# Seven quarter products in place of eight for 68 weight chunks, with weights in rings of 1024 columns

## The chip, the core and the metric

The kernel runs as one program on one NeuronCore of a Trainium2 chip. TensorE (PE) multiplies, VectorE (DVE), ScalarE (ACT) and GpSimd (POOL) do the element work, SyncE (SP) issues the DMAs. The metric is the time of one execution on the device in microseconds, median of several runs: 2743.62 before (2740.0 to 2743.9, 3 runs).

## The reference

One layer of a streaming encoder on x of shape (1, 512, 2048) in float32. Only the products matter here; norms, softmax, convolution and pooling stay as they are.

```python
h = rms_norm(x, norm_mix_pre[l])
z = h @ w_in[l]                              # 2048 x 3328, feeds four mixers A, B, C, D
...                                          # y_a, y_b, y_c, y_d: each mixer, then its own 512 x 2048 map
merged = jax.nn.sigmoid(h @ w_gate[l, 0] + b_gate[l, 0]) * y_a
merged = merged + jax.nn.sigmoid(h @ w_gate[l, 1] + b_gate[l, 1]) * y_b
merged = merged + jax.nn.sigmoid(h @ w_gate[l, 2] + b_gate[l, 2]) * y_c
merged = merged + jax.nn.sigmoid(h @ w_gate[l, 3] + b_gate[l, 3]) * y_d
x = x + rms_norm(merged @ w_o[l], norm_mix_post[l])
h2 = rms_norm(x, norm_ffn_pre[l])
gu = h2 @ w_ffn_in[l]                        # 2048 x 11264
f = (jax.nn.silu(gu[..., :D_FF]) * gu[..., D_FF:]) @ w_ffn_out[l]
x = x + rms_norm(f, norm_ffn_post[l])
```

## The kernel before

Everything is kept transposed: 128 channels on the partitions, the 512 positions on the free axis. A float32 number travels as a pair of float16 numbers, "hi" (rounded) and "lo" (the rest), and a product of two pairs is three float16 matmuls: hi by hi, hi by lo, lo by hi (`three`, lines 1058 to 1063). Each of the three matmuls loads its own 128 x 128 weights, although the first two use the same.

The weights come as **chunks** of 2048 rows by 256 columns, 2 MB in float32: 13 of `w_in`, then for each of 8 pairs of output tiles 4 gate chunks and one chunk of branch weights, 8 of `w_o`, 44 of `w_ffn_in` (each holds 128 gate columns and the 128 up columns that belong to them) and 32 smaller ones of `w_ffn_out` (11 row tiles each). A chunk passes four hands: SP loads it into one of two slots of `stage` (line 249), ACT makes hi (`hi`, line 416), DVE makes lo (`lo`, line 684), PE runs `gemm`: two output tiles of 128 x 512, each 16 row tiles times three matmuls, so 96 matmuls per chunk. ACT may overwrite a weight slot only when PE has finished the chunk before last (`chunk_done`), SP only when lo is made (`lo_ready`).

All waits are semaphores and each engine works its instructions in order. The repeating parts are hardware loops (`Fori`) on every engine: on PE one with 924 matmuls per turn for the pairs 1 to 6 (3 turns of 2 pairs), one with 192 for `w_o` (3 turns), one with 192 for `w_ffn_in` (20 turns of 2 chunks) and one with 264 for `w_ffn_out` (8 turns).

In the gate stage ACT takes the sigmoid out of PSUM, and DVE merges (`merge`, lines 917 and 921): branch product times gate, four added. In the FFN stage DVE scales both tiles (lines 1007 and 1010), ACT takes the silu (line 637), DVE multiplies (line 1017), ACT and DVE split the result into hi and lo (lines 642 and 1024). The two-step norms between the stages are where PE waits for others.

The matmuls themselves and the functions that the diff touches:

## Time and profile before

| | |
|---|---|
| time, median of 3 runs | 2743.62 us (2740.0 to 2743.9) |
| span of the profiled execution | 2739.6 us; the page gives no time of its own around it, the timed runs lie 0.4 to 4.3 us above |
| PE | busy 2693.0 us, 98%, 12452 matmul records |
| PE weight loads | busy 1233.7 us, 45% |
| DVE | busy 1034.3 us, 38% |
| ACT | busy 713.1 us, 26% |
| POOL | busy 105.7 us, 4% |
| HBM | 104 GB/s over the span |
| granted TensorE clock | 0.995 on average |

Engines work beside one another, so the shares don't add up. A matmul record is longer than its place in the pipeline: it is 380 ns for 512 columns while the next one starts 216 ns later, and the distance of two starts is what counts. "Idle before" a group says what the engine waited for.

### The profile page before, as it was taken

The page shows a single profiled execution, that of the slowest core. Times are in us where ns is not written, and L with a number is a line of the kernel's source. Part 1 is how long each engine was busy: PE and PEld are TensorE (multiplying, and loading weights), DVE is VectorE, ACT ScalarE, POOL GpSimd, SP SyncE. Part 2 cuts the span into 40 slices and gives each one's busy share as a digit, 9 for nine tenths or more (in the row PEclk, how much of TensorE's full clock was granted, in tenths as well). Part 3 has the DMA queues.
Part 4 walks back from the last instruction along what each step waited for, and adds up shares of the span by engine and source line. Part 5 has one row for each costly group of instructions (what it writes and reads, how often), then busy time and mean ns, then how long its engine had stood idle before and what let it go on. Part 6 is the DMA issues. An engine that isn't in the chain of part 4 may idle for free.

```text
span 2739.6 us, 28637 instructions
## 1 busy us (share of the span) xinstructions
PE 2693.0 (98%) x12452; PEld 1233.7 (45%) x12452; DVE 1034.3 (38%) x792; ACT 713.1 (26%) x537; POOL 105.7 (4%) x96
## 2 busy tenths in 40 slices
PE   7999999999999999999899999999999999999998
PEld 4444444444444444444444444444444444444443
DVE  8976534323323323321643333333333332222123
ACT  5226322222222222222432222222222222122221
POOL 0000020000000000011400000000000000000002
PEclk9999999999999999999999999999999999999999
DMA  5221222222222223242143223222222312222223
GB/s 227 98 93 62 93 87 106 103 87 108 102 90 97 110 87 117 98 165 106 60 156 122 92 92 114 101 92 103 111 92 95 119 63 106 105 102 90 103 105 122
DMA packets 23108, 286.39 MB, mean 105 GB/s; under 512 B 2560, under 2 KB 2688, under 8 KB 3968
## 3 DMA queue, kind: packets, MB, share of 16 engines
q1 hardware_dynamic: 23040, 285.37, 27.8%
q8 instruction: 57, 0.93, 0.1%
q14 instruction: 11, 0.09, 0.0%
HBM read 276.97 MB, written 8.39 MB: 104 GB/s over the span
## 4 chain that ended last, share of the span: by engine, by line
PE 96%; DVE 2%; issue 1%; ACT 0%; DMA 0%; DVEq 0%; POOL 0%; SPq 0%; ACTq 0%; POOLq 0%
PE psum L1061 31%; PE psum L1063 31%; PE psum L1062 31%; PE psum L1152 1%; PE psum L1177 0%; DVE region_b L982 0%; DVE region_a L971 0%; DVE wlo L694 0%; DVE stage L1049 0%; PE psum L1090 0%; PE psum L1163 0%; DMA region_b<-x_t 0%; DVE region_a L754 0%; DVE region_b L1044 0%; DVE work L743 0%
## 5 line engine op out<-in xcount | busy, mean ns | idle before, releaser
L684 DVE SCALAR_TENSOR_TENSOR wlo<-stage,whi 128x4096 f16<-128x4096 f32 (+2 forms) x133 | 539.7, 4058 | 1073.6 <-ACT whi L416 1073.4
L1061 PE MATMUL psum<-region_a,whi 128*128 128x512 f16 x2352 | 893.2, 380 | 14.1 <-issue 8.8
L1062 PE MATMUL psum<-region_a,whi 128*128 128x512 f16 x2352 | 892.9, 380 | 0.0
L1063 PE MATMUL psum<-region_a,wlo 128*128 128x512 f16 x2352 | 892.9, 380 | 0.0
L1061 PE MATMUL psum<-region_b,whi 128*128 128x512 f16 x1664 | 632.0, 380 | 8.7 <-DVE region_b L982 8.7
L1062 PE MATMUL psum<-region_b,whi 128*128 128x512 f16 x1664 | 631.7, 380 | 0.0
L1063 PE MATMUL psum<-region_b,wlo 128*128 128x512 f16 x1664 | 631.7, 380 | 0.0
L416 ACT ACTIVATE whi<-stage 128x4096 f16<-128x4096 f32 (+2 forms) x133 | 440.6, 3313 | 258.2 <-PE psum L1063 258.2
L1061 PEld LDWEIGHTS psum<-region_a,whi 128*128 128x128 f16 x2352 | 230.4, 98 | 297.9 <-issue 20.7
L1063 PEld LDWEIGHTS psum<-region_a,wlo 128*128 128x128 f16 x2352 | 230.4, 98 | 278.7 <-issue 2.1
L1062 PEld LDWEIGHTS psum<-region_a,whi 128*128 128x128 f16 x2352 | 230.5, 98 | 275.9 <-issue 1.7
L1061 PEld LDWEIGHTS psum<-region_b,whi 128*128 128x128 f16 x1664 | 163.1, 98 | 207.0 <-DVE region_b L982 9.6
L1063 PEld LDWEIGHTS psum<-region_b,wlo 128*128 128x128 f16 x1664 | 163.0, 98 | 197.2 <-issue 1.5
L1062 PEld LDWEIGHTS psum<-region_b,whi 128*128 128x128 f16 x1664 | 163.1, 98 | 196.1 <-issue 1.1
L1010 DVE SCALAR_TENSOR_TENSOR work<-psum,rinv_sb 128x512 f32<-128x512 f32 x44 | 30.4, 691 | 402.2 <-PE psum L1063 402.2
L642 ACT ACTIVATE region_a<-work 128x512 f32 (+1 forms) x44 | 27.7, 629 | 448.4 <-DVE work L1017 448.4
L436 ACT ACTIVATE region_a<-psum,vecs 128x512 f32<-128x512 f32 x32 | 22.0, 687 | 307.6 <-PE psum L1063 307.6
L388 POOL TENSOR_TENSOR std<-std,work 128x512 f32<-128x512 f32 x32 | 41.1, 1284 | 1459.2 <-ACT work L595 1459.2
L817 DVE SCALAR_TENSOR_TENSOR region_b<-region_a,vecs,region_b 128x511 f32<-128x511 f32 (+14 forms) x120 | 91.0, 758 | 4.0
L637 ACT ACTIVATE work<-work 128x512 f32<-128x512 f32 x44 | 27.7, 630 | 225.6 <-DVE work L1007 225.6
L595 ACT ACTIVATE work<-psum 128x512 f32<-128x512 f32 x32 | 19.1, 597 | 214.6 <-PE psum L1063 214.6
L432 ACT ACTIVATE region_a<-psum,vecs 128x512 f32<-128x512 f32 x32 | 22.0, 687 | 201.6 <-PE psum L1063 201.6
(138 smaller groups left out, 762.3 us busy)
## 6 DMA issues: line engine op xcount, KB each, us to landing
stage<-w_ffn_in_chunks SPq DMA_DIRECT2D x44, 2048.0 KB, 7.9
stage<-w_gate_chunks SPq DMA_DIRECT2D x32, 2048.0 KB, 7.7
stage<-w_ffn_out_chunks SPq DMA_DIRECT2D x32, 1408.0 KB, 5.8
stage<-w_in_chunks SPq DMA_DIRECT2D x13, 2048.0 KB, 7.7
stage<-w_o_chunks SPq DMA_DIRECT2D x8, 2048.0 KB, 8.0
stage<-w_branch_chunks SPq DMA_DIRECT2D x8, 1664.0 KB, 6.7
region_b<-x_t SPq DMA_DIRECT2D x4, 1024.0 KB, 7.9
region_a<-x_t SPq DMA_DIRECT2D x2, 2048.0 KB, 9.5
```

The source lines that it names most:

```text
L388: ins = nc.gpsimd.tensor_tensor(std[:, :], std[:, :], work[:, t, :], ALU.add)
L416: nc.scalar.activation(whi[:, n0 % 2, 0:width], stage[:, n0 % 2, 0:width], ACT.Copy, scale=WSCALE).then_inc(hi_ready, 1)
L432: nc.scalar.activation(dst, psum[:, 0, :], func, scale=UNSCALE, **kw).then_inc(evicted0, 1)
L637: nc.scalar.activation(work[:, w, :], work[:, w, :], ACT.Silu, scale=UNSCALE).then_inc(f_silu, 1)
L642: nc.scalar.activation(dst, work[:, w, :], ACT.Copy).then_inc(f_hi, 1)
L684: V.scalar_tensor_tensor(out=wlo[:, n0 % 2, 0:width], in0=stage[:, n0 % 2, 0:width], scalar=WSCALE, in1=whi[:, n0 % 2, 0:width], op0=ALU.m ...
L817: ins = V.scalar_tensor_tensor(out=conv[:, i, q:S], in0=glu[:, i, 0:S - q], scalar=w, in1=conv[:, i, q:S], op0=ALU.mult, op1=ALU.add)
L1010: V.scalar_tensor_tensor(out=work[:, w + 1, :], in0=psum[:, bank + 1, :], scalar=UNSCALE, in1=rinv_sb[:, :], op0=ALU.mult, op1=ALU.mult).t ...
L1061: mm(psum[:, bank, :], high, hk[0], start=start, stop=False)
L1062: mm(psum[:, bank, :], high, hk[1], start=False, stop=False)
L1063: return mm(psum[:, bank, :], wlo[:, slot, w_at:w_at + P], hk[0], start=False, stop=stop)
L1152: last = mm(psum[:, 2 + p // 2, (p % 2) * 2 * P + k0:(p % 2) * 2 * P + 2 * P], query[half, p, m * P:m * P + P], key[half, (m - 1) * P + k0 ...
```

## The change

The eight products of a 2 x 2 by 2 x 2 block multiplication are replaced by seven (Strassen's scheme in Winograd's form) for the gate chunks of pairs 1 to 7 (28) and for the FFN-in chunks 4 to 43 (40). A chunk is cut into four **quarters** of 1024 rows by 128 columns (one for each half of the rows, taken alternately, and each output tile); the activations are cut by the same halves of the rows and by halves of the positions (256). One product is then 8 row tiles times three matmuls of 128 x 256: 24 matmuls, and 168 per chunk where 96 of 128 x 512 stood.

DVE makes four sums of weight quarters in float32 in the stage buffers, in place (`make_s3`, `make_s2`, `make_s1`, `make_s4`), and each of the seven operands is then split into hi and lo as a **unit** of 1024 columns. The sums of the activations (`tset`, four sets of 8 tiles) are made once, while the four gate chunks of pair 0 and the first FFN chunks run (`h_sums`, `x_sums`, `t_low`; ACT's `t_high`). Two products are added up in PSUM by not starting anew; what is needed before the next product is added, ACT copies out (`keep_product`, three times 128 x 256 per chunk), and DVE puts the four quarters of the result together (`c22_c21`, `c11`, `c12`). ACT takes sigmoid or silu afterwards from SBUF.

`stage` is now a ring of 8 quarters (0.5 MB each, as much as before in all); hi and lo lie in a ring of 4 units (`wq`, half of what there was), so ACT's hi of a unit waits until PE has finished the unit four before (`unit_done`). The branch products follow each gate chunk, not all four, and are merged one at a time. DVE, ACT, POOL and SP programs are written out without loops. On PE the loops have 1500 matmuls per turn (pairs 2 to 7, 3 turns), 672 (FFN-in chunks 4 to 43, 10 turns of 4 chunks) and 264 (`w_ffn_out`, 8 turns); `w_o` is written out.

PE, one row tile of an FFN-in chunk in the loop, both output tiles before, one product now (names: output <- moving operand, weights; 128 partitions x columns):

```order
L1061 MATMUL psum<-region_b,whi 128x512
L1062 MATMUL psum<-region_b,whi 128x512
L1063 MATMUL psum<-region_b,wlo 128x512
L1061 MATMUL psum<-region_b,whi 128x512
L1062 MATMUL psum<-region_b,whi 128x512
L1063 MATMUL psum<-region_b,wlo 128x512
```

```order
L1346 MATMUL psum<-region_t,wq 128x256
L1347 MATMUL psum<-region_t,wq 128x256
L1348 MATMUL psum<-region_t,wq 128x256
L1517 REGISTER_ALU
L1518 REGISTER_ALU
L1346 MATMUL psum<-region_t,wq 128x256
L1347 MATMUL psum<-region_t,wq 128x256
L1348 MATMUL psum<-region_t,wq 128x256
```

Every matmul streams half the columns; the two register instructions stand between two products and prepare the values of the waits.

DVE, one FFN-in chunk in the loop before (line 684 is lo of a whole chunk):

```order
L684 SCALAR_TENSOR_TENSOR wlo<-stage,whi 128x4096
L1004 REGISTER_ALU
L1007 TENSOR_TENSOR work<-psum,rinv_sb 128x512
L1010 SCALAR_TENSOR_TENSOR work<-psum,rinv_sb 128x512
L1016 REGISTER_ALU
L1017 TENSOR_TENSOR work<-work 128x512
L1024 ISA
L1024 TENSOR_TENSOR region_a<-work,region_a 128x512
```

and a stretch of one chunk now, from the sum `make_s3` for the next chunk to the copying out of the last quarter (line 808 is lo of a unit, 825, 831 and 836 are weight sums, 846 to 855 the result's quarters):

```order
L825 TENSOR_TENSOR stage<-stage 128x1024
L808 SCALAR_TENSOR_TENSOR wq<-stage,wq 128x1024
L846 TENSOR_TENSOR work<-psum,work 128x256
L847 TENSOR_TENSOR work<-psum,work 128x256
L808 SCALAR_TENSOR_TENSOR wq<-stage,wq 128x1024
L831 TENSOR_TENSOR stage<-stage 128x1024
L851 TENSOR_TENSOR work<-psum,work 128x256
L1303 SCALAR_TENSOR_TENSOR work<-work,rinv_sb 128x512
L808 SCALAR_TENSOR_TENSOR wq<-stage,wq 128x1024
L836 TENSOR_TENSOR stage<-stage 128x1024
L855 TENSOR_TENSOR work<-psum,work 128x256
L1310 TENSOR_TENSOR work<-work,rinv_sb 128x512
```

Where five operations stood per chunk there are 19: seven of line 808, four weight sums, four quarters of the result and four of 512 columns.

The core of the diff:

```diff
+STAGES, RING = 8, 4
+SU = 7
...
+PLAIN_FFN = 4
+X_SIZES = (8, 8, 7, 7, 7, 7)
...
+def strassen_units(cs):
+    u, q = len(UNIT_AT), len(FREED)
+    UNIT_AT.extend((q, q + 2, q + 2, q, q + 1, q + 3, q + 3))
+    UNIT_SUMS.extend((0, 0, 4 * cs + 2, 4 * cs + 3, 4 * cs + 1, 0, 4 * cs + 4))
+    UNIT_W.extend((UW,) * SU)
+    FREED.extend((u + 4, u + 5, u + 7, u + 7))
...
+            def load(q, src, width=UW):
+                if q >= STAGES:
+                    sp.wait_ge(lo_ready, FREED[q - STAGES])
+                sp.dma_start(stage[:, q % STAGES, 0:width], src).then_inc(landed[q % STAGES], 16)
...
+            def hi(u):
+                q = UNIT_AT[u]
+                if UNIT_SUMS[u]:
+                    act.wait_ge(sums_made, UNIT_SUMS[u])
+                else:
...
+                nc.scalar.activation(dst, stage[:, q % STAGES, 0:UNIT_W[u]], ACT.Copy, scale=WSCALE).then_inc(hi_ready, 1)
...
+            def keep_product(u, cs, i):
+                act.wait_ge(unit_done, DONE[u])
+                if cs >= 1:
+                    act.wait_ge(c_read, 4 * (cs - 1) + (3, 4, 2)[i])
+                nc.scalar.activation(copies[:, i, :], psum[:, Q1, 0:HS], ACT.Copy).then_inc(copied, 1)
...
+            def ffn_chunk(c):
+                u, cs = U_FS + SU * (c - PLAIN_FFN), CS_F + c - PLAIN_FFN
+                keep_product(u, cs, 0)
+                hi(u + 4)
+                silu(c - 1)
+                hi(u + 5)
+                keep_product(u + 2, cs, 1)
+                hi(u + 6)
+                f_high(c - 1)
+                hi(u + 7)
+                keep_product(u + 4, cs, 2)
+                hi(u + 8)
+                hi(u + 9)
+                hi(u + 10)
...
+            def lo(u):
...
+                dve.wait_ge(hi_ready, u + 1)
+                V.scalar_tensor_tensor(out=slot[:, 1, 0:w], in0=stage[:, q % STAGES, 0:w], scalar=WSCALE,
+                                       in1=slot[:, 0, 0:w], op0=ALU.mult, op1=ALU.subtract).then_inc(lo_ready, 1)
...
+            def make_s3(u, cs):
+                a, c, d, b = quarters(u)
+                for q in (UNIT_AT[u], UNIT_AT[u] + 1):
+                    dve.wait_ge(landed[q % STAGES], 16 * (q // STAGES + 1))
+                V.tensor_tensor(c, a, c, ALU.subtract).then_inc(sums_made, 1)
+            def make_s2(u, cs):
+                a, c, d, b = quarters(u)
+                dve.wait_ge(lo_ready, u + 2)
+                dve.wait_ge(sums_made, 4 * cs + 1)
+                V.tensor_tensor(d, d, c, ALU.subtract).then_inc(sums_made, 1)
+            def make_s1(u, cs):
+                a, c, d, b = quarters(u)
+                dve.wait_ge(sums_made, 4 * cs + 2)
+                V.tensor_tensor(a, a, d, ALU.add).then_inc(sums_made, 1)
+            def make_s4(u, cs):
+                a, c, d, b = quarters(u)
+                dve.wait_ge(lo_ready, u + 6)
+                V.tensor_tensor(b, b, d, ALU.subtract).then_inc(sums_made, 1)
+            def c22_c21(u, cs):
+                dve.wait_ge(unit_done, DONE[u + 3])
+                dve.wait_ge(copied, 3 * cs + 3)
+                V.tensor_tensor(cb[:, 1, 0:HS], psum[:, Q3, 0:HS], copies[:, 2, :], ALU.add).then_inc(c_read, 1)
+                V.tensor_tensor(cb[:, 1, HS:S], psum[:, Q2, 0:HS], copies[:, 2, :], ALU.add).then_inc(c_read, 1)
+            def c11(u, cs):
+                dve.wait_ge(unit_done, DONE[u + 5])
+                V.tensor_tensor(cb[:, 0, HS:S], psum[:, Q4, 0:HS], copies[:, 0, :], ALU.add).then_inc(c_read, 1)
+            def c12(u, cs):
+                dve.wait_ge(unit_done, DONE[u + 6])
+                V.tensor_tensor(cb[:, 0, 0:HS], psum[:, Q3, 0:HS], copies[:, 1, :], ALU.add).then_inc(c_read, 1)
...
+            def sum_halves(t):
+                V.tensor_tensor(t[:, 2, :], t[:, 0, :], t[:, 2, :], ALU.subtract).then_inc(dve_step, 1)
...
+                V.tensor_tensor(t[:, 3, :], t[:, 3, :], t[:, 1, :], ALU.subtract).then_inc(t_made, 1)
...
+            def t_low(i, t, done):
+                dve.wait_ge(t_hi, done)
+                V.tensor_tensor(tset[:, :, i, 1, :], t, tset[:, :, i, 0, :], ALU.subtract).then_inc(t_lo, 1)
...
+            def ffn_chunk(c):
+                u, cs = U_FS + SU * (c - PLAIN_FFN), CS_F + c - PLAIN_FFN
+                following = (u + SU, cs + 1) if c + 1 < FT else None
+                lo(u + 4)
+                lo(u + 5)
+                make_s4(u, cs)
+                f_product(c - 1)
+                lo(u + 6)
+                f_low(c - 1)
+                if following:
+                    make_s3(*following)
+                lo(u + 7)
+                dve.wait_ge(f_lo, c)
+                c22_c21(u, cs)
+                lo(u + 8)
+                if following:
+                    make_s2(*following)
+                c11(u, cs)
+                dve.wait_ge(c_read, 4 * cs + 2)
+                V.scalar_tensor_tensor(out=cb[:, 1, :], in0=cb[:, 1, :], scalar=UNSCALE, in1=rinv_sb[:, :],
+                                       op0=ALU.mult, op1=ALU.mult).then_inc(f_up, 1)
+                lo(u + 9)
+                if following:
+                    make_s1(*following)
+                c12(u, cs)
+                dve.wait_ge(c_read, 4 * cs + 4)
+                V.tensor_tensor(cb[:, 0, :], cb[:, 0, :], rinv_sb[:, :], ALU.mult).then_inc(f_gate, 1)
+                lo(u + 10)
...
+            def three_half(bank, w, w_at, x, start, stop):
+                to = psum[:, bank, 0:HS]
+                mm(to, w[:, 0, w_at:w_at + P], x[:, 0, :], start=start, stop=False, skip_group_check=True)
+                mm(to, w[:, 0, w_at:w_at + P], x[:, 1, :], start=False, stop=False, skip_group_check=True)
+                return mm(to, w[:, 1, w_at:w_at + P], x[:, 0, :], start=False, stop=stop, skip_group_check=True)
...
+            def product(u, bank, x, start):
+                for i in range(KP):
+                    last = three_half(bank, wq[:, u % RING], i * P, x(i), start and i == 0, i == KP - 1)
+                last.then_inc(unit_done, 1)
+            def strassen(s, u, cs, first=False, units=0, chunks=0, turn=None):
+                pe.wait_ge(lo_ready, at(u + 1, units, turn))
+                if not first:
+                    pe.wait_ge(copied, at(3 * cs, 3 * chunks, turn))
+                product(u, Q1, lambda i: s[:, 1, 0, i], True)
+                pe.wait_ge(lo_ready, at(u + 2, units, turn))
+                if not first:
+                    pe.wait_ge(c_read, at(4 * cs - 2, 4 * chunks, turn))
+                product(u + 1, Q2, lambda i: tset[:, 3, i], True)
+                pe.wait_ge(lo_ready, at(u + 3, units, turn))
+                pe.wait_ge(copied, at(3 * cs + 1, 3 * chunks, turn))
+                product(u + 2, Q1, lambda i: tset[:, 1, i], False)
+                pe.wait_ge(lo_ready, at(u + 4, units, turn))
+                if not first:
+                    pe.wait_ge(c_read, at(4 * cs, 4 * chunks, turn))
+                product(u + 3, Q3, lambda i: tset[:, 2, i], True)
+                pe.wait_ge(lo_ready, at(u + 5, units, turn))
+                pe.wait_ge(copied, at(3 * cs + 2, 3 * chunks, turn))
+                product(u + 4, Q1, lambda i: tset[:, 0, i], False)
+                pe.wait_ge(lo_ready, at(u + 6, units, turn))
+                product(u + 5, Q4, lambda i: s[:, 1, 1, i], True)
+                pe.wait_ge(lo_ready, at(u + 7, units, turn))
+                pe.wait_ge(c_read, at(4 * cs + 1, 4 * chunks, turn))
+                product(u + 6, Q3, lambda i: s[:, 0, 1, i], False)
...
+            def pair_stage(jj, first=False, pairs=0, turn=None):
+                for j in range(4):
+                    u, cs = U_G + GU * (jj - 1) + (SU + 1) * j, CS_G + 4 * (jj - 1) + j
+                    strassen(h, u, cs, first and j == 0, GU * pairs, 4 * pairs, turn)
+                    pe.wait_ge(lo_ready, at(u + SU + 1, GU * pairs, turn))
+                    pe.wait_ge(y_used, at(2 * (4 * jj + j), 8 * pairs, turn))
+                    branch(u + SU, j, jj // 2, turn)
+            pe.wait_ge(t_lo, KP)
+            pair_stage(1, first=True)
             with pe.Fori(0, 3) as turn:
-                pair_stage(C_G + 5, E_G + 4, 1, 10, turn)
-                pair_stage(C_G + 10, E_G + 8, 2, 10, turn)
-            pair_stage(C_G + 35, E_G + 28, 7)
...
```

## Rows read from the trace of the kernel before

**Rows 1.** The page: busy time, the chain that ended last, weight queue and instruction queues.

```profile
span 2739.6 us, 28637 instructions
PE 2693.0 (98%) x12452; PEld 1233.7 (45%) x12452; DVE 1034.3 (38%) x792; ACT 713.1 (26%) x537; POOL 105.7 (4%) x96
...
q8 instruction: 57, 0.93, 0.1%
...
PE 96%; DVE 2%; issue 1%; ACT 0%; DMA 0%; DVEq 0%; POOL 0%; SPq 0%; ACTq 0%; POOLq 0%
```

**Rows 2.** Groups by form: line engine op, names, shapes, count | busy us, mean ns.

```profile
L427 ACT ACTIVATE whi<-stage 128x1024 f16<-128x1024 f32 x16 | 16.0, 1044 | 0.0
...
L1044 DVE TENSOR_TENSOR region_b<-region_b,psum 128x1024 f32<-128x1024 f32 x6 | 7.1, 1212 | 1.5 <-PE psum L1102 1.5
```

**Rows 3.** Timeline of PE in the FFN loop: start us, us, engine, line.

```profile
1700.19 0.38 PE L1063 MATMUL psum<-region_b,wlo 128*128 128x512 f16 x1
1700.19 0.10 PEld L1061 LDWEIGHTS psum<-region_b,whi 128*128 128x128 f16 x1
1700.41 0.38 PE L1061 MATMUL psum<-region_b,whi 128*128 128x512 f16 x1
```

**Rows 4.** Timeline of DVE in the FFN loop, one period.

```profile
1707.08 0.69 DVE L1007 TENSOR_TENSOR work<-psum,rinv_sb 128x512 f32<-128x512 f32 x1
1717.44 0.69 DVE L1010 SCALAR_TENSOR_TENSOR work<-psum,rinv_sb 128x512 f32<-128x512 f32 x1 [9.67 <-PE psum L1063]
...
1719.96 0.69 DVE L1024 TENSOR_TENSOR region_a<-work,region_a 128x512 f32 x1 [1.00 <-ACT region_a L642]
1723.25 4.42 DVE L684 SCALAR_TENSOR_TENSOR wlo<-stage,whi 128x4096 f16<-128x4096 f32 x1 [2.60 <-ACT whi L416]
1727.80 0.69 DVE L1007 TENSOR_TENSOR work<-psum,rinv_sb 128x512 f32<-128x512 f32 x1
```

**Rows 5.** Timeline of PE: weight loads with short matmuls behind them.

```profile
18.81 0.86 PEld L1095 LDWEIGHTS psum<-ones,std 128*128 128x128 f32 x7
...
363.31 1.50 PE L1219 MATMUL psum<-wst,region_b 128*128 128x128 f32 x12
```

**Rows 6.** Durations of line 1219, ns min/median/max.

```profile
L1219 PEld LDWEIGHTS psum<-wst,region_b x32: 190/192/192, 363.1 to 366.7; 128*128 128x128 f32 x32
L1219 PE MATMUL psum<-wst,region_b x32: 272/275/275, 363.3 to 366.8; 128*128 128x128 f32 x32
```

**Rows 7.** Timeline of DVE: 1024 columns alone and back to back.

```profile
41.24 1.22 DVE L694 SCALAR_TENSOR_TENSOR wlo<-stage,whi 128x1024 f16<-128x1024 f32 x1
...
46.16 4.62 DVE L694 SCALAR_TENSOR_TENSOR wlo<-stage,whi 128x1024 f16<-128x1024 f32 x4
...
1352.63 2.24 DVE L974 TENSOR_TENSOR region_a<-region_a 128x1024 f32<-128x1024 f32 x1
```

**Rows 8.** Timeline of PE and PEld where the 924-matmul loop turns back.

```profile
645.09 0.38 PE L1063 MATMUL psum<-region_a,wlo 128*128 128x512 f16 x1
...
649.60 0.61 PE L1061 MATMUL psum<-region_a,whi 128*128 128x512 f16 x1 [4.13 <-issue]
...
849.96 0.10 PEld L1063 LDWEIGHTS psum<-region_a,wlo 128*128 128x128 f16 x1
855.21 0.10 PEld L1061 LDWEIGHTS psum<-region_a,whi 128*128 128x128 f16 x1 [5.15 <-issue]
```

**Rows 9.** Windows there: us, PE, PEld, DVE, ACT, POOL busy, granted clock, DMA.

```profile
650.00:655.00 5.00, 5.00 (x19) 2.08 (x18) 2.99 (x1) 1.98 (x1) 0.00 (x0) 0.76 0.01 3
...
855.00:860.00 5.00, 4.79 (x12) 1.72 (x13) 2.91 (x1) 2.06 (x1) 0.00 (x0) 0.50 0.01 3
```

**Rows 10.** DMA queues from 645 to 850 us, one turn: packets, MB.

```profile
q8 instruction: 10, 0.16, 0.3%
```

**Rows 11.** DMA queues from 1450 to 2250 us, some 19 turns of the FFN-in loop.

```profile
q8 instruction: 1, 0.02, 0.0%
```

**Rows 12.** DMA queues from 2200 to 2700 us, the `w_ffn_out` loop.

```profile
q8 instruction: 2, 0.03, 0.0%
```

1156 lines of the change are left out of this document (672 added, 484 removed).

## The prediction

> **What bounds the kernel now.** I read the page first: PE is busy for 2693.0 of 2739.6 us, no other engine for more than 38%, and 96% of the chain that ended last is PE [rows 1]. Then the timeline of PE: in the stages that the change touches the matmuls of 512 columns start 0.22 us apart, and the next weight load begins with the matmul that runs and ends after 0.10 us, well inside it [rows 3]. The timeline of DVE gives the exact period: line 1007 starts at 1707.08 and again at 1727.80, so an FFN-in chunk takes 20.72 us, which is 96 matmuls of 215.8 ns [rows 4]. In that period DVE works 7.2 us and waits for the rest. The kernel is bound by the number of columns that PE streams, at the granted clock of the upper level (2.4 GHz, 0.995 on average). So a change that takes columns away saves what it takes, as long as three things hold: the matmul of half the length starts after half the time, DVE's new work fits beside PE, and PE's new loops turn without a stall. I price them in this order.
>
> **PE per chunk.** At 2.4 GHz 512 columns take 213.3 ns, so 2.5 ns of the 215.8 are fixed. A matmul of 256 columns is then 106.7 + 2.5 = 109.2 ns. Seven products of 24 are 168 matmuls: 168 x 0.1092 = 18.34 us against 20.72, which saves 2.38 us. With 28 gate and 40 FFN-in chunks that is 68 x 2.38 = 162 us. The trace has no float16 matmul of 256 columns. The lower end is half of today's distance, 107.9 ns (18.13 us, 176 us saved). The upper end is from the float32 rows: seven weight loads before matmuls of one column take 0.86 us, so they start (0.86 - 0.19) / 6 = 111 ns apart, and the twelve matmuls of line 1219, each with fresh weights, also start (1.50 - 0.275) / 11 = 111 ns apart [rows 5, 6]. Such a load is recorded with 192 ns, twice the 98 of a float16 load, so a float16 load should not limit below 111 ns: 18.65 us, 141 us saved. I take 109.2; the rest of PE's matmuls (branches, `w_in`, `w_o`, `w_ffn_out`) are the same in number and length.
>
> There is a rule that speaks against this. Rows 3 show that a load adds nothing to a distance of 216 ns. The Trainium skill (TensorE: Matmul & The Clock Gate, section Back-to-back issue gap) says that in a stream of load and matmul pairs both set the distance: about 81 ns at 128 columns where the columns alone need 56, and 131 ns at 512. The 131 doesn't agree with the 216 of this trace. Its 25 ns on top at 256 columns, an estimate from that page, would make 134 ns and a chunk of 22.5 us, longer than now; that is the slower rival below.
>
> **DVE per FFN-in chunk.** Seven lo and four weight sums of 1024 columns: one alone is 1.22 us, but four in a row take 4.62, so one follows the other after (4.62 - 1.22) / 3 = 1.13 us [rows 7]; 11 x 1.13 = 12.5. Reads of 256 columns from PSUM: 0.69 us for 512 [rows 4] and 1.21 for 1024 [rows 2] give 0.43; four are 1.7. Four operations of 512 at 0.69 are 2.8. Together 17.0 us. Where an operation waits for the one just before it the overlap of 0.09 is lost and some 0.04 added; if all did, it would be 11 x 1.26 + 4 x 0.47 + 4 x 0.73 = 18.7. On top come three places where lo needs ACT's hi of a sum that DVE has only just made: 1.04 us of hi [rows 2], covered in part by 0.6 to 0.9 us of other DVE work in between, so some 1.1 us a chunk. The ends are 17.0 and 19.8 us; I take 18.2, just under PE's 18.34, because only about four of the 19 operations wait for their predecessor. GpSimd is idle here; where it works, line 974 has taken up to 2.24 us in place of 1.21 [rows 7], so this holds only as long as it stays idle.
>
> The order of the waits matters more than the sum. PE's seventh product adds onto the bank that `c22_c21` must have read by 6 x 2.62 = 15.7 us of the chunk. The way there starts when the second product is done (5.4 us): hi 1.04, lo 1.26, `make_s4` 1.26, hi 1.17, lo 1.13, `f_low` 0.7, `make_s3` 1.13, lo 1.13, then the read 0.43, which ends at 14.7. One microsecond is left. Units are ready 3 us or more before PE wants them. In the gate stage DVE has 15.9 us in a chunk of 18.34 + 5.2 us (24 branch matmuls), except after branch C, which has 6: there the merge and `merged_low` push the read about 0.5 us past its time, 6 times, 3 us.
>
> ACT has 7 x 1.04 + 3 x 0.4 + 1.3 = 9.8 us a chunk and DMA the same bytes as before in pieces of 0.5 MB, 2 MB per 18.3 us, where 1.1 times today's rate is wanted; both at no cost, and the cover is wide.
>
> **Once only.** Before the first Strassen chunk PE waits for the last `t_low`: eviction, hi, lo and the pair 1.2 behind each other are 4.4 us after the gate tile, and branch C covers 1.3: 3 us. Before `w_o` the last merge, two copies on ACT and two `merged_low` end 7.1 us after branch C, and PE wants the last one at 4.5: 2.6 us. The sums for the FFN (25 us on DVE) run beside chunks 1 to 3 with nearly all of DVE used: 2 us. With the 3 us above, 11 us. Before, none of these stalls was there.
>
> **Loops.** When PE's loop of 924 matmuls turned back, nothing ran from 645.09 to 649.60 and from 849.96 to 855.21, and then the granted clock was 0.76 and 0.50 in the stretch of 5 us that follows, the lower level of 1.2 GHz for a part of it [rows 8, 9]. That is 4.3 + 1.2 and 5.0 + 2.5, on average 6.5 us. In that turn the instruction queue moved 10 packets of 16 KB [rows 1, 10]; in 19 turns of 192 matmuls it moved one, in 7 of 264 two [rows 11, 12], and there is no stall. So a body that is still held turns for nothing. The gate loop is longer now but turns twice as before: no difference. The FFN-in loop had 192 and has 672 matmuls and 9 turns back. By length it is 672 / 924 of nine packets, that is 7, with the one fetched ahead 8. The ends are 0 (it is held) and 9 x 6.5 = 58 us. [...]
>
> The Trainium skill (Runtime: NRT & Kernel Launch, section Instruction fetch mechanics) gives PE a store of 128 KiB, eight such blocks, which would just hold this loop; the same section warns that a jump outside a window of two blocks must be fetched. The 264-matmul loop is longer than two blocks and doesn't stall, so the second rule doesn't hold here; the first is not tested by any row between 264 and 924.
>
> **Sum.** 2739.6 - 162 + 11 = 2589 us of span. The runs lie 4.0 us (median) above the span, so 2593.
>
> **Rivals.**
> 1. The FFN-in loop isn't held. For it: the nearest row in length stalls. Against: the count above. Time: 2593 + 58 = 2651, with gaps of some 5 us every 73 us, and the clock low behind each.
> 2. DVE becomes the bound of the 40 FFN-in chunks. For it: 91% and more of its time is used and the way to the seventh product has 1 us left. At the upper end of 19.8 us a chunk it costs 1.46 x 40 = 58 us, in the middle 28: 2621.
> 3. Slower than before: the weight load of 98 ns isn't hidden any more. It begins when the running matmul begins [rows 3]; 118 ns are left today for the hand-over, then 11. If the hand-over takes H after the load, the distance is 98 + H, and above 20.72 / 168 = 123 ns, H above 25, the change loses. At H = 36 a chunk is 22.5 us: 2743.6 + 68 x 1.8 + 11 = 2877. Against it: rows 5 and 6, where a load twice as long follows every 111 ns.
> 4. Two of the small losses together (distance 111 ns, 21 us more; DVE; longer gaps between the stages) leave a gain of under 60 us: 2690 to 2740.
>
> **How the numbers follow.** Forecast 0.50 (its own range 2579 to 2622, from 107.9 to 111 ns and with up to 8 us more for the stalls), rival 1 0.24, rival 2 0.16, rival 3 0.07, rival 4 0.03. The range of 2580 to 2665 leaves out the slower case, the fourth and the lowest tip of the first. About 5 us or 0.2% is what a measurement of this kernel tells from no change. Faster by more: 0.92; within 0.01; slower 0.07.
>
> **What would show it.** PE records of 256 columns about 109 ns apart, 18.3 us from one line 1303 to the next in the FFN stage; DVE busy above 85% there and PE without waits for DVE; the instruction queue nearly still over the FFN-in loop; loop gaps only twice, in the gate stage. I am wrong if the distance is above 111 ns, if PE waits at line 846's read in each chunk, or if gaps of issue come every 73 us.

## The result

The changed kernel takes 2607.6 us (median of 4 runs, 2606.0 to 2609.3) against 2743.1 us (4 runs, 2740.0 to 2743.9) for the kernel before. The ratio is 0.951, with a 95% interval of 0.9495 to 0.9522: 5% faster. Forecast were 2593 us, with a range of 2580 to 2665. The direction, the mechanism and the likeliest case came out; the time was forecast 14.6 us too low, through stalls where one stage hands over to the next.

### The profile page after: what moved, and what is told of

Read it like the earlier page. It is cut to its first block, busy times and chain, and to the rows that moved or that the text cites. A ratio compares the mean times of both kernels' runs of the same rounds, so it can differ in the third digit from the quotient of the medians.

```text
span 2607.6 us, 41323 instructions
## 1 busy us (share of the span) xinstructions
PE 2536.9 (97%) x17348; PEld 1711.9 (66%) x17348; DVE 1775.5 (68%) x1962; ACT 1070.3 (41%) x1311; POOL 118.0 (5%) x96
## 4 chain that ended last, share of the span: by engine, by line
PE 86%; DVE 7%; issue 3%; ACT 2%; POOL 0%; DMA 0%; DVEq 0%; SPq 0%; ACTq 0%; POOLq 0%
PE psum L1346 15%; PE psum L1347 15%; PE psum L1348 15%; PE psum L1339 13%; PE psum L1340 13%; PE psum L1341 13%; DVE wq L808 1%; ACT wq L460 1%; PE psum L1418 1%; PE psum L1443 1%; DVE region_f L1192 0%; DVE region_t L869 0%; DVE region_f L1180 0%; DVE region_f L1089 0%; DVE std L901 0%
## 5 line engine op out<-in xcount | busy, mean ns | idle before, releaser
L808 DVE SCALAR_TENSOR_TENSOR wq<-stage,wq 128x1024 f16<-128x1024 f32 (+2 forms) x668 | 801.7, 1201 | 687.3 <-ACT wq L460 681.9
L460 ACT ACTIVATE wq<-stage 128x1024 f16<-128x1024 f32 (+2 forms) x668 | 691.0, 1036 | 922.4 <-PE psum L1341 512.7
L1339 PE MATMUL psum<-region_f,wq 128*128 128x512 f16 x1616 | 615.4, 381 | 30.0 <-DVE work L1214 9.5
L1340 PE MATMUL psum<-region_f,wq 128*128 128x512 f16 x1616 | 615.1, 381 | 0.0
L1341 PE MATMUL psum<-region_f,wq 128*128 128x512 f16 x1616 | 615.0, 381 | 0.0
L1348 PE MATMUL psum<-region_t,wq 128*128 128x256 f16 x2176 | 593.6, 273 | 0.0
L1346 PE MATMUL psum<-region_t,wq 128*128 128x256 f16 x2176 | 593.5, 273 | 0.0
L1347 PE MATMUL psum<-region_t,wq 128*128 128x256 f16 x2176 | 593.5, 273 | 0.0
L1346 PE MATMUL psum<-region_f,wq 128*128 128x256 f16 x1632 | 446.3, 273 | 14.8 <-DVE region_t L869 8.9
L1347 PE MATMUL psum<-region_f,wq 128*128 128x256 f16 x1632 | 446.3, 273 | 0.0
L1348 PE MATMUL psum<-region_f,wq 128*128 128x256 f16 x1632 | 446.3, 273 | 0.0
L1339 PEld LDWEIGHTS psum<-region_f,wq 128*128 128x128 f16 x1616 | 158.1, 98 | 225.1 <-issue 15.8
L1341 PEld LDWEIGHTS psum<-region_f,wq 128*128 128x128 f16 x1616 | 158.2, 98 | 192.4 <-issue 2.5
L1340 PEld LDWEIGHTS psum<-region_f,wq 128*128 128x128 f16 x1616 | 158.1, 98 | 185.9 <-issue 1.7
L1346 PEld LDWEIGHTS psum<-region_t,wq 128*128 128x128 f16 x2176 | 212.5, 98 | 25.1
L1347 PEld LDWEIGHTS psum<-region_t,wq 128*128 128x128 f16 x2176 | 212.4, 98 | 25.2
L1348 PEld LDWEIGHTS psum<-region_t,wq 128*128 128x128 f16 x2176 | 212.4, 98 | 25.1
L1346 PEld LDWEIGHTS psum<-region_f,wq 128*128 128x128 f16 x1632 | 159.8, 98 | 39.2 <-DVE region_t L869 9.4
L632 ACT ACTIVATE work<-psum 128x256 f32<-128x256 f32 x204 | 77.4, 379 | 236.4 <-PE psum L1348 236.4
L1347 PEld LDWEIGHTS psum<-region_f,wq 128*128 128x128 f16 x1632 | 159.8, 98 | 21.9
L1348 PEld LDWEIGHTS psum<-region_f,wq 128*128 128x128 f16 x1632 | 159.7, 98 | 19.3
L427 POOL TENSOR_TENSOR std<-std,work 128x512 f32<-128x512 f32 x32 | 54.1, 1691 | 1361.6 <-ACT work L667 1361.6
```

Source lines behind the costliest of these rows:

```text
L427: ins = nc.gpsimd.tensor_tensor(std[:, :], std[:, :], squares[:, t, :], ALU.add)
L460: nc.scalar.activation(dst, stage[:, q % STAGES, 0:UNIT_W[u]], ACT.Copy, scale=WSCALE).then_inc(hi_ready, 1)
L632: nc.scalar.activation(copies[:, i, :], psum[:, Q1, 0:HS], ACT.Copy).then_inc(copied, 1)
L808: V.scalar_tensor_tensor(out=slot[:, 1, 0:w], in0=stage[:, q % STAGES, 0:w], scalar=WSCALE, in1=slot[:, 0, 0:w], op0=ALU.mult, op1=ALU.sub ...
L1339: mm(to, w[:, 0, w_at:w_at + P], x_hi, start=start, stop=False)
L1340: mm(to, w[:, 0, w_at:w_at + P], x_lo, start=False, stop=False)
```

## The profile after

The page of the changed kernel, to be held against [rows 1]: the span, busy times, the total of the queue that brings instructions, and the chain that ended last.

```profile
span 2607.6 us, 41323 instructions
PE 2536.9 (97%) x17348; PEld 1711.9 (66%) x17348; DVE 1775.5 (68%) x1962; ACT 1070.3 (41%) x1311; POOL 118.0 (5%) x96
...
q8 instruction: 79, 1.29, 0.2%
...
PE 86%; DVE 7%; issue 3%; ACT 2%; POOL 0%; DMA 0%; DVEq 0%; SPq 0%; ACTq 0%; POOLq 0%
```

PE is still the engine of the chain, but its share fell from 96 to 86%, and DVE has 7%. That is the first sign of something that the period of a chunk doesn't show. The timeline of PE inside an FFN-in chunk (start us, us, engine, line), where [rows 3] had 0.22 us from one matmul to the next:

```profile
1717.42 0.27 PE L1348 MATMUL psum<-region_f,wq 128*128 128x256 f16 x1
1717.53 0.27 PE L1346 MATMUL psum<-region_f,wq 128*128 128x256 f16 x1
1717.64 0.27 PE L1347 MATMUL psum<-region_f,wq 128*128 128x256 f16 x1
1717.75 0.27 PE L1348 MATMUL psum<-region_f,wq 128*128 128x256 f16 x1
```

The matmuls of 256 columns start 0.11 us apart. The timeline of DVE over the same chunk answers to [rows 4]:

```profile
1709.99 1.23 DVE L841 TENSOR_TENSOR stage<-stage 128x1024 f32<-128x1024 f32 x1
...
1712.34 1.22 DVE L808 SCALAR_TENSOR_TENSOR wq<-stage,wq 128x1024 f16<-128x1024 f32 x1 [0.52 <-ACT wq L460]
...
1716.35 0.42 DVE L846 TENSOR_TENSOR work<-psum,work 128x256 f32<-128x256 f32 x1
...
1719.74 0.68 DVE L1303 SCALAR_TENSOR_TENSOR work<-work,rinv_sb 128x512 f32<-128x512 f32 x1
...
1728.33 1.23 DVE L841 TENSOR_TENSOR stage<-stage 128x1024 f32<-128x1024 f32 x1
```

Line 841 is the weight sum `make_s4`, once a chunk. From one line 841 to the next it is 18.34 us, to the hundredth the forecast of 168 x 0.1092; over 34 chunks the mean is 18.340. The window over 350 us of that stage (us, then PE, PEld, DVE, ACT and POOL busy, granted clock, DMA share, GB/s) says how full it is:

```profile
1450.00:1800.00 350.00, 350.00 (x3209) 313.05 (x3207) 323.29 (x363) 177.14 (x231) 0.00 (x0) 1.00 0.34 114
```

PE never stops, DVE is busy for 92%, which is 16.94 us of each 18.34. So the time that is missing isn't in the chunks. The list of PE's waits (who waited for whom: us, times, longest) has it:

```profile
PE psum L1339 <- DVE work L1214: 9.5, 2, 9.2
PE psum L1346 <- DVE region_t L869: 8.9, 1, 8.9
...
PE psum L1346 <- issue: 4.3, 2, 2.3
PE psum L1339 <- issue: 3.7, 1, 3.7
PE psum L1339 <- DVE region_f L1100: 3.0, 1, 3.0
...
PE psum L1339 <- DVE wq L808: 1.7, 1, 1.7
PE psum L1346 <- DVE work L846: 1.6, 4, 0.4
```

Where they lie shows the timeline of PE, of which these are all rows with an idle time above 1.7 us from pair 0's end to the end of FFN-in, the norm stage left out:

```profile
437.75 0.38 PE L1339 MATMUL psum<-region_f,wq 128*128 128x512 f16 x1 [1.74 <-DVE wq L808]
...
451.94 0.38 PE L1339 MATMUL psum<-region_f,wq 128*128 128x512 f16 x1 [3.68 <-issue]
...
462.27 0.40 PE L1346 MATMUL psum<-region_f,wq 128*128 128x256 f16 x1 [8.87 <-DVE region_t L869]
...
738.64 0.28 PE L1346 MATMUL psum<-region_f,wq 128*128 128x256 f16 x1 [2.05 <-issue]
...
922.06 0.28 PE L1346 MATMUL psum<-region_f,wq 128*128 128x256 f16 x1 [2.28 <-issue]
...
1110.70 0.39 PE L1339 MATMUL psum<-region_f,wq 128*128 128x512 f16 x1 [2.98 <-DVE region_f L1100]
...
1367.58 0.61 PE L1339 MATMUL psum<-region_f,wq 128*128 128x512 f16 x1 [9.21 <-DVE work L1214]
```

Three gaps stand together where pair 0 ends (14.3 us), one of 9.2 us between the third and the fourth plain FFN-in chunk. Behind the long ones the granted clock is at the lower level for a while (windows, columns as above):

```profile
460.00:465.00 5.00, 2.73 (x13) 1.94 (x14) 5.00 (x6) 0.77 (x1) 0.00 (x0) 0.50 0.08 19
465.00:470.00 5.00, 5.00 (x38) 4.07 (x36) 2.09 (x3) 2.48 (x4) 0.00 (x0) 0.78 0.22 86
...
740.00:745.00 5.00, 5.00 (x49) 4.46 (x47) 4.89 (x8) 3.33 (x5) 0.00 (x0) 1.00 0.30 105
...
1365.00:1370.00 5.00, 2.42 (x6) 0.87 (x7) 3.32 (x5) 3.11 (x4) 0.00 (x0) 0.50 0.32 106
```

From the start of PE at 462.27 us to 470 us 49 matmuls started where 71 of 0.109 us would have fitted: 2.4 us lost, and 2.1 behind the gap at 1367 us in the same way. Behind the gap of 2.05 us at 738.6 the clock stayed at its upper level, and nothing was lost.

The sums of a norm (line 1095 before, 1368 now) stand at the same place in both kernels. The starts of their first weight loads cut the span into stretches:

| stretch | before, us | after, us | difference | forecast |
|---|---|---|---|---|
| start | 18.7 | 19.7 | +1.0 | 0 |
| `w_in`, gates, `w_o` | 1306.3 | 1254.5 | -51.9 | -58.0 |
| norm, first two FFN-in chunks | 51.0 | 53.2 | +2.2 | 0 |
| the other FFN-in chunks, `w_ffn_out` | 1338.0 | 1254.7 | -83.4 | -93.2 |
| end | 25.6 | 25.6 | 0 | 0 |
| span | 2739.6 | 2607.6 | -132.1 | -151.2 |

The forecast column is 28 and 40 times 2.38 us less the stalls that the prediction put there (8.6 and 2 us). So 19.1 us of the span are unforecast, and the last 4 that the prediction added for what lies around the span came out as nothing, since the profiled run (2609.3 us) was the slowest of the four.

## The experiments

All times are medians, with the kernel before timed beside them (2741.1 to 2742.3 us). Spans are those of the profiled execution.

### The first place: GpSimd's windows

DVE's timeline at the end of pair 0 in the changed kernel shows two waits in line 1053, where DVE takes up the moving sums (windows) that GpSimd makes for branch C:

```profile
416.68 1.29 DVE L1053 SCALAR_TENSOR_TENSOR region_f<-work,region_f 128x512 f32<-128x512 f32 x2
421.82 0.69 DVE L1053 SCALAR_TENSOR_TENSOR region_f<-work,region_f 128x512 f32<-128x512 f32 x1 [3.85 <-POOL work L403]
427.67 0.69 DVE L1053 SCALAR_TENSOR_TENSOR region_f<-work,region_f 128x512 f32<-128x512 f32 x1 [5.17 <-POOL work L403]
```

GpSimd may make windows three and four only when DVE has used the first two. The kernel before has the same two waits, but there DVE had stood idle for 9.77 us shortly before them, and the wait cost nothing:

```profile
392.03 4.43 DVE L684 SCALAR_TENSOR_TENSOR wlo<-stage,whi 128x4096 f16<-128x4096 f32 x1 [9.77 <-ACT whi L416]
...
401.51 0.69 DVE L886 SCALAR_TENSOR_TENSOR region_a<-work,region_a 128x512 f32<-128x512 f32 x1 [3.85 <-POOL work L361]
407.37 0.69 DVE L886 SCALAR_TENSOR_TENSOR region_a<-work,region_a 128x512 f32<-128x512 f32 x1 [5.17 <-POOL work L361]
```

```diff
-                if k == 31:
-                    for g, w in enumerate(POOL_WINDOWS):
+                if k in (29, 31):
+                    for g, w in list(enumerate(POOL_WINDOWS))[k - 29:k - 27]:
```

> DVE adds the first two of GpSimd's windows to c_x at task 29 instead of 31, so that GpSimd can make windows three and four while DVE does other work. Changed kernel: DVE waits 3.85 + 5.17 us for GpSimd between 418.0 and 427.7 us and everything behind it in its order (halves' sums, t_low, weight lo) is late by that. Theory A (the 1.7 + 3.7 + 8.9 us that PE idles between 436 and 462 us, and the slow clock behind it, come from these 9 us of DVE): the wait for the last t_low falls from 8.9 to about 1 us or nothing, the two gaps before it vanish, the clock stays at the upper level; span and time fall by 12 to 16 us, to 2592 to 2596. Rival B (DVE has too much work in pair 0 whatever GpSimd does): the three gaps shrink by less than 4 us in all, time 2603 to 2608. Rival C (ACT's order of hi and t_high is what is late): DVE's idle time moves to waits for ACT, PE's gaps stay, time 2605 to 2609.

Measured: 2604.0 us (2600.8 to 2605.4), span 2601.6, against 2607.6 for both. The waits for GpSimd are gone, and so are the gaps before 437.75 and 451.94 us. The third stayed: 8.0 us in place of 8.9. Theory A had said that all three came from the 9 us; two did. The last `t_low` was late for another reason, and the time is in rival B's range, although the gaps shrank by 6.3 us and not by less than 4. The stretch from `w_in` to `w_o` is 5.0 us shorter.

### The second place: the eviction of a plain chunk

In DVE's timeline line 1214 of plain chunk 2 runs at 1366.84, though PE's last matmul of that chunk started at 1358: in between stand two halves' sums, a `t_low` and two weight lo, in the order in which they were written.

```diff
             x_low(4)
+            evict_ffn(2)
             x_sums(5)
...
             lo(u + 6)
-            evict_ffn(2)
             x_low(6)
```

> The eviction of plain FFN-in chunk 2 moves in DVE's order from behind the seventh halves' sum to behind the fifth lo of t (three sums, one t lo and two weight lo earlier). Theory A: PE idles 9.2 us before 1367.6 us only since this eviction stands behind 8 us of DVE work that nobody wants yet; now it comes at once, PE's gap there falls to about 0.7 us, the slow clock behind it (10 us at the lower level) goes with it, and the work put back doesn't make the first Strassen chunk late (DVE has 3.5 us without work between 1377 and 1381). Time falls by 9 to 11 us, to 2597 to 2599. Rival B: the work is only late somewhere else: a new wait for weight lo or for the last t_low of at least 5 us shows before the first Strassen FFN chunk, time 2603 to 2608.

Measured: 2597.7 us (2596.9 to 2599.4), 10 us less, span 12.5 less; the wait is 0.9 us, the clock behind it stays up, and no new wait comes before the first Strassen chunk. Theory A. The stretch of the other FFN-in chunks is 10.3 us shorter; the rest of the span's 12.5 lies in the start and the end, which the edit doesn't touch.

> Both moves. Theory A: the two places are 900 us apart and have nothing in common, so the gains add: 21 to 27 us, time 2581 to 2587, and the granted clock is at the upper level from 30 to 1276 us. Rival B for each as told for it alone.

Both together: 2591.6 us (2590.4 to 2593.8), 16.0 less. By the medians the two alone make 3.6 + 9.9 = 13.5, by the spans 6.0 + 12.5 = 18.5 (16.2 together), so they add up within the scatter of some 2 us. By the stretches it is plainer: 5.0 and 10.3 us alone, 5.7 and 10.3 together. The 21 to 27 us that were expected didn't come, because the 8.0 us of the last `t_low` were still there. The clock didn't stay up either: it was at the lower level for 10 us behind that wait and for 3.4 us where `w_o` starts.

### What else stood at the first place

Where DVE's order in the last chunk of pair 0 has the last `t_low` at its end, the sums were spread: three in chunk 0, one in chunk 3.

```diff
-                t_low(2 * j, t_h, 2 * j + 1)
-                h_sums(2 * j + 1)
+                t_low(i, t_h, i + 1)
+                if j < 3:
+                    h_sums(i + 1)
...
+                if j == 0:
+                    h_sums(2)
                 lo(B + 8)
+                if j == 0:
+                    t_low(2, t_h, 3)
```

> On top of both moves (e3, 2591.6 us): of the eight halves' sums with their t_low in pair 0, three are made in chunk 0 and one in chunk 3 instead of two and two. In e3 PE still waits 8.0 us for the last t_low, which stands at 453.4 us behind c_lo, the other t_low, the last sums and the two weight sums S2 and S1. Theory A (what is left of the wait is the order in chunk 3: the last t_low has 6.9 us of DVE work ahead of it that nobody wants yet): the last t_low is made at about 445.5 us, before PE asks at 446.7; the wait and the 10 us of slow clock behind it go: 9 to 11 us less, 2581 to 2583. Rival B (pair 0 has too much DVE work in all, 33 us of sums): chunk 0 or 1 gets late instead, PE waits there for weight lo or c_lo: time 2586 to 2592.

Measured: 2592.3 us (2590.6 to 2593.0): nothing gained, and the stretch from `w_in` to `w_o` is even 2.7 us longer than with both moves, 1.2 of it in the two turns of the gate loop. The timeline of PE says why:

```profile
410.63 0.38 PE L1349 MATMUL psum<-region_f,wq 128*128 128x512 f16 x1 [1.72 <-DVE wq L811]
...
450.68 0.59 PE L1349 MATMUL psum<-region_f,wq 128*128 128x512 f16 x1 [3.62 <-issue]
...
461.90 0.27 PE L1356 MATMUL psum<-region_t,wq 128*128 128x256 f16 x1 [3.06 <-ACT work L635]
```

The one wait of 8.0 us became three of 8.4 us together. The work that was moved made PE wait earlier, at 410 us. Branch C waits for `c_lo`, which ends at 450.58 behind a weight lo. And the third product waits for ACT's copy of the first one, which stands behind `merged_high`, which waits for DVE's merge. Rival B was nearer than A. The next kernel takes up the last two; `tasks(34)` is `c_lo` now:

```diff
-                if k == 33:
+                if k == 34:
...
                 lo(B + 4)
+                if j == 3:
+                    tasks(34)
                 h_sums(i)
...
-            merged_high(0)
             for jj in range(1, PAIRS):
...
-                if j == 0 and jj >= 2:
+                if j == 0:
                     merged_high(jj - 1)
```

and puts the last `t_low` ahead of one weight lo.

> On top of e10 (2592.3 us), whose profile shows two gaps where pair 0 ends: 3.6 us before branch C (c_lo stands on DVE behind a weight lo that waits for ACT) and 3.1 us before the third product (ACT's copy of the first product stands behind merged_high, which waits for DVE's last merge). Here c_lo goes ahead of the last sums, t_low(7) ahead of one weight lo, and merged_high(0) behind ACT's copy and one hi of the first Strassen chunk. Theory A (three orders were stacked at one place, each hid the next): all gaps between 430 and 465 us are under 1 us together, no stretch of slow clock there, time 6 to 9 us less, 2583 to 2586. Rival B (the dependencies themselves are too long there): a gap of 2 us or more comes at another of the first three products: 2588 to 2592.

Measured: 2587.0 us (2586.8 to 2590.9), 5 less. Of the waits 3.4 us for the last `t_low` remain, at 451.78, and the 1.7 at 410.6. So both theories hold in part: three orders were stacked there, and something is left under them. It isn't shown that DVE has too much to do. From 380 to 450 us it works 46.3 of the 70 us in the changed kernel and 57.3 in the last kernel below, and there it still waits 13.3 us, seven times, for ACT's hi, as in these rows of ACT and DVE:

```profile
432.20 1.06 ACT L596 ACTIVATE region_t<-region_f 128x1024 f16<-128x1024 f32 x1 [6.92 <-DVE region_f L867]
...
433.74 1.99 ACT L460 ACTIVATE wq<-stage 128x1024 f16<-128x1024 f32 x2
...
434.81 1.22 DVE L810 SCALAR_TENSOR_TENSOR wq<-stage,wq 128x1024 f16<-128x1024 f32 x1 [2.64 <-ACT wq L460]
```

ACT makes `t_high` (line 596) ahead of that hi, and `t_high` waits for the halves' sums that DVE has only just made. The wait of 1.7 us at 410.6 also follows such a lo. This is rival C of the first experiment, ACT's order; no run here moves the hi ahead of `t_high`.

### PE's loops

Two kernels change the length of a loop's body in the changed kernel and nothing else. The first writes the gate loop out (`for jj in range(2, PAIRS): pair_stage(jj)`).

> PE's gate loop (3 turns of two pairs) written out, everything else as in the changed kernel. Theory A: the idle 2.05 us at 738.6 and 2.28 us at 922.1 are the fetch of the loop's first block of code, and straight code is fetched ahead, so both go and nothing replaces them: time 4 to 5 us less, 2603. Rival B: straight code of 6 pairs is fetched too slowly (28 KB a chunk) and PE waits for code in every pair: time 2610 or more, with waits of issue spread over the gate stage.

Measured: 2605.9 us (2604.9 to 2606.0), span 2603.2. Both gaps of issue are gone (4.3 us), and 1.4 us came back as waits for line 846. The stretch from `w_in` to `w_o` is 2.9 us shorter, which is 4.3 less 1.4. The span fell by 4.4 us; the medians differ by 1.7, which the intervals of the two ratios (0.9491 to 0.9517 and 0.9495 to 0.9522) don't tell apart. The second makes the FFN-in loop as long as the gate loop:

```diff
-            with pe.Fori(0, (FT - PLAIN_FFN) // 4) as turn:
-                for c in range(4):
-                    strassen(h2, U_FS + SU * c, CS_F + c, False, 4 * SU, 4, turn)
+            with pe.Fori(0, (FT - PLAIN_FFN) // 8) as turn:
+                for c in range(8):
+                    strassen(h2, U_FS + SU * c, CS_F + c, False, 8 * SU, 8, turn)
```

> The changed kernel with PE's FFN-in loop as 5 turns of 8 chunks (1344 matmuls) in place of 10 turns of 4 (672). Theory A (the loop of 672 turns without a stall because its code is still held, by its size): at 1344 matmuls, as long as the gate loop, each of 4 turns back costs an idle of about 2.2 us as at 738.6 and 922.1 us, issue as what ends it, and the instruction queue moves 11 to 12 packets in each turn in place of nearly none: 9 us slower, 2616 to 2618. Rival B (in the FFN stage turning back is hidden whatever the length): no gap of issue, no difference.

Measured: 2621.1 us (2620.0 to 2624.8), 13.5 slower. Each of the four turns back shows two gaps, here the first of them:

```profile
1536.63 0.28 PE L1346 MATMUL psum<-region_f,wq 128*128 128x256 f16 x1 [1.71 <-DVE wq L808]
...
1539.97 0.27 PE L1346 MATMUL psum<-region_f,wq 128*128 128x256 f16 x1 [1.86 <-issue]
```

The weight lo that the first row names had ended at 1536.1, 0.5 us before PE went on, and in the second row, 12 matmuls later, nothing is named: both read as PE waiting for code, for the block that the loop jumps to and for the one behind it. It is 3.4 us a turn where 2.2 were expected, which is the second gap that the expectation didn't count. From 1545 to 1690 us, most of one turn, the queue of instructions moved 12 packets:

```profile
q8 instruction: 12, 0.20, 0.6%
```

The changed kernel moved 2 in the 640 us from 1440 to 2080, which are eight turns and a half:

```profile
q8 instruction: 2, 0.03, 0.0%
```

So a loop of 672 matmuls is held and one of 924 or more isn't. The Trainium skill (Runtime: NRT & Kernel Launch, section Instruction fetch mechanics) gives PE a store of 128 KiB, filled in blocks of 16 KiB, which makes eight blocks. By that rule 672 matmuls, some 7 blocks, are held and 1344 not, and this agrees with the packets above. Where between 672 and 924 matmuls the limit lies no run shows.

### How near DVE is to being the bound

An idle sum of 1024 columns (on numbers that nobody uses) is added to each FFN-in chunk on DVE, once ahead of the read of `c22` and `c21`, and in another kernel twice at the end of the chunk.

```diff
                 lo(u + 7)
+                V.tensor_tensor(extra, some, some, ALU.subtract)
                 dve.wait_ge(f_lo, c)
                 c22_c21(u, cs)
```

> The changed kernel with one idle sum of 1024 columns (1.13 us, nobody uses it) more per FFN-in chunk on DVE, just ahead of the read of c22 and c21. In the changed kernel the read ends 14.4 us after the chunk's start and PE wants it at 15.7; DVE works 16.94 of 18.34 us. Theory A (PE sets the period, DVE has 1.4 us and the way to the seventh product 1.3 us left): both are just enough, the period stays 18.34 to 18.4 us: time 2607 to 2610. Rival B (DVE's waits for ACT can't be used, the order has no slack): the period grows by the whole 1.13 us, 45 us in all, 2653.

> The changed kernel with two such idle sums per FFN-in chunk at the end of its order on DVE. Theory A (the period is the larger of PE's 18.34 us and DVE's sum): DVE's work becomes 16.94 + 2.26 = 19.2 us, above 18.34, so the period becomes 19.2 to 19.6 us (where waits for ACT remain): 34 to 50 us slower, 2642 to 2658. Rival B (the whole 2.26 us go on top): 90 us slower, 2698. Rival C (DVE has more room than its busy time says): under 10 us.

Measured: 2641.0 us (2639.0 to 2642.1) with one, 2671.7 (2670.3 to 2675.3) with two. The periods are 19.18 and 20.03 us. PE's timeline in each, one row of the period's single wait:

```profile
1711.51 0.28 PE L1360 MATMUL psum<-region_f,wq 128*128 128x256 f16 x1 [0.67 <-DVE work L848]
```

```profile
1707.31 0.28 PE L1360 MATMUL psum<-region_f,wq 128*128 128x256 f16 x1 [1.52 <-DVE work L848]
```

Theory A failed with one sum: PE doesn't set the period any more, and 33 us were lost where none was expected. With two its mechanism held and its size didn't: 20.03 us a chunk in place of 19.2 to 19.6, and 64 us. DVE's slack is not 18.34 - 16.94 = 1.4 us. In the kernel with one sum, 0.95 us of each period are three waits of DVE for ACT's hi (0.24, 0.52 and 0.19 us), the last two of them for the hi of a sum that DVE itself has just made, and the added sum fills none of them. What is left is 18.34 + 1.13 - 19.18 = 0.3 us of 1.4. With two sums it is 18.34 + 2.26 - 20.03 = 0.6 us, since the wait of 0.24 is gone there. Nor was the whole added sum lost, as rival B had it.

### What a matmul costs with a load before each

One kernel uses 128 of the 256 columns in each Strassen matmul and leaves the other half out.

> The changed kernel with 128 columns instead of 256 in each Strassen matmul (the second 128 of each quarter are left out), each still with its own weight load. Theory A (distance is columns / 2.4 GHz + 2.5 ns, the load is hidden): 55.8 ns apart within a product. Rival B (the load of 98 ns as recorded is the floor and 256 columns stood just above it): 98 to 107 ns apart, so the changed kernel had 2 to 11 ns to spare. Rival C (in between: a load takes less than it is recorded with): 60 to 80 ns. In either case DVE's 18.0 us a chunk in the FFN stage are then the bound where PE is quicker: the FFN chunk takes 17.8 to 18.1 us, and the whole 2570 to 2600.

Its timeline of PE:

```profile
1702.33 0.22 PE L1346 MATMUL psum<-region_t,wq 128*128 128x128 f16 x1
1702.38 0.22 PE L1347 MATMUL psum<-region_t,wq 128*128 128x128 f16 x1
...
1703.56 0.22 PE L1347 MATMUL psum<-region_t,wq 128*128 128x128 f16 x1
1703.61 0.22 PE L1348 MATMUL psum<-region_t,wq 128*128 128x128 f16 x1
```

From 1702.33 to 1703.61 it is 23 matmuls: 55.7 ns each, 53.3 for the columns and 2.4 fixed. Theory A: the load isn't seen even here, so 256 columns stood far above any limit of it, and the recorded 98 ns of a load are not its price. Every matmul here has its load, so what the 2.4 ns are, and whether a load has a part in them, no run shows. Before these rows the matmuls were 107 ns apart at the lower level of the clock. The Trainium skill (TensorE: Matmul & The Clock Gate, section Back-to-back issue gap) has 81 ns at 128 columns; this row doesn't agree. The period of an FFN-in chunk became 18.05 us (line 1303 at 1700.39, 1718.45 and 1736.51): that is DVE's own pace, now that PE is quicker, and in the range that was expected. The one run took 2545.6 us, below the 2570 to 2600 expected.

### All together

The last two kernels put all of it together: windows, eviction, spread sums, orders, the gate loop written out, and each half of the last merge waited for by itself before `w_o` (`pe.wait_ge(m_lo, 2 * i + 1 + r)`).

> e11 with PE's gate loop written out and, before w_o, PE's first tile waiting for each half of a pair's merged_low by itself. Theory A: the two gaps of issue (4.3 us) go and about 1.4 us come back as waits for the read of the second product after branch C, as in e4; the wait before w_o falls from 3.0 to 2.4: 3 to 4 us less than e11. Rival B: as the median of e4 lay only 1.7 us below the changed kernel, the gain is under 2 us.

Measured: 2585.0 us (2583.6 to 2586.4), 2 less than before the last two edits: rival B's side. PE waits 2.4 us before `w_o`, and 3.9 us (7 times) for line 848, of which 0.9 in the first Strassen chunk.

```diff
+                if j == 3:
+                    t_low(i, t_h, i + 1)
                 lo(B + 5)
```

> On top of e12 (2585.0 us): the last t_low of pair 0 also goes ahead of the weight lo that waits 1.5 us for ACT. In e11 and e12 PE still waits 3.4 us for it, until 451.8. Theory A: t_low is made at about 449.2 us, PE waits under 1.5 us, and the stretch of slow clock behind goes: 2 to 4 us less, 2581 to 2583. Rival B: the weight lo it overtakes is wanted at the same moment (it is the first product's), so the wait only changes its name: 2584 to 2586.

Measured: 2584.0 us (2582.1 to 2585.3), ratio to before 0.9424 (0.9411 to 0.9437). The wait at the first Strassen product:

```profile
450.78 0.37 PE L1363 MATMUL psum<-region_f,wq 128*128 128x256 f16 x1 [2.36 <-DVE wq L810]
```

3.4 us for `t_low` became 2.4 us for the weight lo that it overtook: rival B. The stretch from `w_in` to `w_o` is 1.2 us shorter, while the two ranges of times overlap, so the medians alone don't tell the two kernels apart. Apart from the kernel that leaves columns out this one has the lowest median, 23.6 us under the changed kernel and 157 under the one before.

## Why the prediction was right, and where not

- **PE per chunk** (109.2 ns, 18.34 us, 162 us saved): shown, 18.340 us over 34 chunks. The term that carries the forecast had no error to speak of. That the fixed part is 2.4 to 2.5 ns at 128, 256 and 512 columns alike the kernel with 128 columns shows. The slower rival with 98 + H is refuted by the same rows.
- **DVE per FFN-in chunk** (18.2 us, of which 1.1 waits for hi): 18.05 us when PE doesn't hold it, 16.94 of them busy. The read that PE's seventh product waits for (line 846) ends at 1716.77, which is 14.6 us after the chunk's start (its second product starts at 1704.76, one product of 2.62 us later), where 14.7 was forecast. Rival 2 did not happen, by 0.3 us a chunk. The kernels with idle sums show what it would have cost: 33 us for one, 64 for two.
- **Loops** (FFN-in held, two gaps in the gate stage): shown; the loop of twice the length costs 13.5 us more. The forecast took nothing for the FFN-in loop, and no row of before showed that; the runs do, with no gap and 2 packets in 640 us. A part was wrong: "no difference" for the gate loop. Its gaps were 4.1 and 4.7 us in PE's own rows (the prediction read 5.0 for the second, from the rows of the weight loads) and are 2.05 and 2.28 now, and no stretch of slow clock follows. With [rows 9]'s 1.2 and 2.5 us that is 8.2 us better than forecast. How much of this comes again in each kernel is open: with the sums spread, the clock was at the lower level for 3.4 us behind a gap of 2.2.
- **Once only** is the step that failed. The prediction said "Before the first Strassen chunk PE waits for the last `t_low`: ... 3 us". It was 14.3 us of gaps at that place and 2.4 us of slow clock. And "The sums for the FFN (25 us on DVE) run beside chunks 1 to 3 with nearly all of DVE used: 2 us" was 9.2 us and 2.1 of clock. The first was counted as dependencies, operation behind operation, as if DVE were free when each became ready, the second as a load, as if only DVE's sum counted. DVE runs its list in order. What stood ahead in the list were GpSimd's two windows, `c_lo`, the weight sums, the next halves' sums, most of them not wanted yet; the runs with the windows and the eviction moved show 16 us of it. Of the other two small terms one was near, 3.0 us before `w_o` (2.6 forecast), and one was half, 1.6 after branch C (3 forecast).
- **The sum.** Of 19.1 us of span: gates +16.7 - 3 at the first Strassen chunk, +0.4 - 1.4 for the small terms, -8.2 for the loops, which is 4.5 of the 6.1 in the table; FFN 11.3 - 2 = 9.3 of 9.8. The start (+1.0) is open; it lay between 18.5 and 19.6 us in the experiments without any change to it.
- **The norm stage** (+2.2) is read from the timelines alone, the first row before and the second now; no run tests it:

```profile
1326.58 1.16 PE L1102 MATMUL psum<-ident,irms 128*128 128x128 f32 x8 [0.47 <-DVE irms L701]
```

```profile
1276.80 2.08 PE L1374 MATMUL psum<-ident,irms 128*128 128x128 f32 x8 [1.60 <-DVE irms L873]
```

These matmuls wait for a short ACT and a short DVE operation behind the sums of the norm. DVE's started 1.3 us behind the start of the sums before and 2.4 us now: ACT was done with its weight hi when the sums ended, and now works on them for 1.0 us longer. Then the eight matmuls run at the lower level of the clock (0.62 granted from 1275 to 1280 us, where before it was 1.00 at the same place), 0.9 us longer. Together that is some 2.0 of the 2.2 us.
- **Luck** had a part in how near the forecast came. The stalls at the hand-overs cost some 22 us more than the 11 forecast, while "up to 8 us more" was allowed for them; the gate loop's turns gave back 8.2. That 2607.6 us still lies in the case's own range of 2579 to 2622 is because its upper end had room for a distance of 111 ns, which didn't come.
